# Second mixer of an encoder: queries, keys and values by seven products of half matrices

## The chip, the cores and the metric
One core of a Trainium2 chip runs the whole program. The metric is the device time of one execution in microseconds. Five instruction streams work side by side: PE (TensorE), DVE (VectorE), ACT (ScalarE), POOL (GpSimd) and SP (SyncE, which here only issues DMAs). Each runs its own instructions in order, and semaphores tie them together.

## What is computed
Two token sequences of 512 and 256 tokens (plus 16 meta tokens each, so T = 800 columns) go through two layers: an mLSTM mixer and a SwiGLU network, then a differential attention mixer and a second SwiGLU network. The part that matters here is the attention mixer (8 heads, two components of 64 each):

```python
proj = xn @ w_in                                  # xn = rmsnorm(h), 1024 -> 3 * 1024
q = proj[..., :1024].reshape(B, L, 8, 2, 64); k = proj[..., 1024:2048].reshape(B, L, 8, 2, 64)
v = proj[..., 2048:].reshape(B, L, 8, 128)
q = partial_rope(_rms_f32(q, g_q), cos, sin) * 64 ** -0.5
k = partial_rope(_rms_f32(k, g_k), cos, sin)
p = softmax(q @ k.T);  a = p[:, :, 0] - lam * p[:, :, 1]
o = _rms_f32(a @ v, g_sub) * (1.0 - lambda_init)
h = h + o @ w_out
```

All matrices are float32. The kernel writes each as a rounded high part plus a low part and makes every product three times (high by high, high by low, low by high).

## The kernel before
Activations lie transposed in on-chip memory: `h` holds the residual as 8 tiles of 128 features by 800 tokens. `xh`, `xl` are the high and low parts of the normalised input, `wh`, `wl` those of a block of weights, `sx` the operands of the SwiGLU products. SwiGLU networks (`ffn`) already multiply by a seven-product scheme on half matrices: a product of two halves feeds two outputs, sums of weights are formed in DRAM ahead of time by copies (SP, `copy_for_sum`) and accumulating DMAs (POOL, `add_for_sum`), and sums of activations by DVE. The matmuls of these products are those of L974. `ORDER` is the list of the network's products; the last 28 of the first network belong to four output jobs a, b, c, d of 9 matmuls a product, and DVE adds each to `h` (`add_out`, L1715). When a tile of `h` is complete, ACT writes `xh` and a square (`high_and_square`, L2384, L2387), DVE writes `xl` and adds the square to a running sum (`low_and_squares`, L1624, L1631).

The second mixer is made of 24 blocks, numbered from `MIX1`: for each head a block of keys, one of queries, one of values (`attn_cols`). A block (`run_block`, matmuls on L884, those of the first block on L1408) is 8 feature tiles times 3 part products times 2 column groups, 48 matmuls: 400 + 400 columns for keys and values, 512 + 256 for queries. SP loads 512 KB of weights for a block, POOL rounds them (L774) and subtracts (L778). `sum_squares(3)` (L899) sums the squares of a token over the features, `invert(3)` (L1502) gives `rstd`, and `evacuate` and `evacuate_inner` (L1478, L1493) multiply it in as they take a block out of PSUM.

`head` exists on PE, DVE and ACT. For head hd PE computes the scores of six query tiles (`attn_scores`, L1280, L1285), turns the probabilities (`turn_attention`, L1302) and multiplies them by the values (`attend`, L1312). Scores are always made one tile ahead, and the blocks of head hd + 1 are cut into pieces of whole feature tiles (6 matmuls each) and laid between these steps (`beside`, 13 places). DVE takes the maximum of a score tile (`maxima`, L2077), ACT the exponentials (`exps`, L2659), DVE combines the two components (`combine`, L2091). In the second half of a head DVE also rotates the queries of the next head (`rope_start`, `rope_end`, L2034 to L2046), scales its keys (`normalise_k`, L2072) and scales the outputs (L2105); `turn_key_roots` (L1244) on PE and the scores of the next head's first tile wait for that. In head 7 the places are filled with output blocks (`OUT1`). Heads 1 to 6 run in a hardware loop of two heads a turn.

## Time and profile before

| | |
|---|---|
| median of three executions | 1862.98 us (1862.71 to 1864.3) |
| span of the profiled execution | 1860.4 us |
| PE busy | 1849.7 us, 99% of the span |
| DVE, ACT, POOL busy | 1235.1, 879.7, 1162.6 us |
| granted TensorE clock | 1.000 in the whole span |
| end of the first SwiGLU network on PE | 905.64 us after the span's start |
| first scores of the mixer (head 0) on PE | 938.06 us |
| one head of the loop | 48.35 us |

Busy time of an engine is the time in which it executes something; PE's matmuls overlap in the trace, since the end of one is drawn after the start of the next, so the pace of PE is read from start to start. The time of day inside the program is given as us from the span's start. A wait of an engine is in square brackets behind a row, with what ended it.

### The profile page before, as it was taken

To read this page: it belongs to the slowest core of one execution; us is meant where nothing else is said; L and a number is where in the kernel's file an instruction comes from. 1 tells how busy PE (TensorE), PEld (TensorE's weight loads), DVE (VectorE), ACT (ScalarE), POOL (GpSimd) and SP (SyncE) were. 2 spreads that over 40 slices of the span, in tenths; PEclk is the share of its full clock that TensorE was granted. 3 is DMA by queue.
4 is the path that set the end of the run, shared out by engine and by line. 5 is a ranking of instruction groups with operands and counts; after the bars stand their busy time and mean duration, and the time that the engine had idled before them with its cause. 6 is when DMAs were issued, how large, how long until landed. Compare 5 with 4: busy or idle time off the path is not lost.

```text
span 1860.4 us, 31456 instructions
## 1 busy us (share of the span) xinstructions
PE 1849.7 (99%) x10845; PEld 1742.0 (94%) x10845; DVE 1235.1 (66%) x2072; ACT 879.7 (47%) x1855; POOL 1162.6 (62%) x1533
## 2 busy tenths in 40 slices
PE   9999999999999999999999999999999999999999
PEld 8888889999999999999988888888889999999998
DVE  6756566768576757576876666666587575756663
ACT  6444343455444445454444444444465454444553
POOL 4453644468687878788843333333558788887885
PEclk9999999999999999999999999999999999999999
DMA  8789997549697977774475666664233535353534
GB/s 270 257 240 237 222 259 173 183 108 228 209 237 238 235 227 218 250 232 118 107 145 121 126 124 124 130 118 91 74 90 110 148 99 157 100 153 101 154 112 133
DMA packets 380153, 309.51 MB, mean 166 GB/s; under 512 B 14395, under 2 KB 322398, under 8 KB 379766
## 3 DMA queue, kind: packets, MB, share of 16 engines
q1 hardware_dynamic: 349472, 237.81, 42.1%
q0 software_dynamic: 28416, 69.21, 20.5%
q8 instruction: 73, 1.20, 0.3%
q10 hardware_dynamic: 2134, 0.82, 0.2%
q14 instruction: 58, 0.48, 0.1%
HBM read 302.16 MB, written 144.04 MB: 240 GB/s over the span
## 4 chain that ended last, share of the span: by engine, by line
PE 91%; DVE 5%; ACT 1%; issue 1%; DMA 1%; POOL 0%; SPq 0%; ACTq 0%; DVEq 0%; POOLq 0%
PE ps L974 51%; PE ps L884 26%; PE ps L1155 3%; PE ps L1312 3%; PE ps L1280 2%; PE ps L1302 1%; PE ps L1130 1%; PE ps L1214 1%; DVE rstd L1502 1%; PE ps L1164 1%; DVE sx L1554 0%; PE ps L1244 0%; DVE mx L2077 0%; DVE gt L1661 0%; DMA wk<-in_x_prompt_dram 0%
## 5 line engine op out<-in xcount | busy, mean ns | idle before, releaser
L974 PE MATMUL ps<-sx,wh 128*128 128x400 f32 (+1 forms) x2044 | 530.3, 340 | 0.9 <-POOL wl L808 0.5
L808 POOL TENSOR_TENSOR wl<-raw,wh 128x256 fp32r<-128x256 f32 (+1 forms) x432 | 355.6, 855 | 97.9 <-ACT wh L2243 96.4
L774 POOL CAST wh<-raw 128x256 fp32r<-128x256 f32 x248 | 102.5, 456 | 450.6 <-PE ps L884 424.9
L974 PEld LDWEIGHTS ps<-sx,wh 128*128 128x128 f32 x2044 | 373.4, 188 | 3.0 <-ACT gt_first L2258 0.9
L974 PE MATMUL ps<-sx,wl 128*128 128x400 f32 (+1 forms) x1022 | 347.6, 340 | 0.0
L808 POOL TENSOR_TENSOR wl<-raws,wh 128x256 fp32r<-128x256 f32 x328 | 283.8, 910 | 84.4 <-ACT wh L2243 84.0
L1715 DVE TENSOR_TENSOR h<-h,ps 128x400 f32<-128x400 f32 (+1 forms) x280 | 154.5, 559 | 131.5 <-PE ps L974 131.4
L974 PE MATMUL ps<-fx,wh 128*128 128x400 f32 (+1 forms) x904 | 235.3, 341 | 0.1
L884 PE MATMUL ps<-xh,wh 128*128 128x512 f32 (+1 forms) x752 | 211.2, 357 | 0.0
L884 PE MATMUL ps<-xl,wh 128*128 128x512 f32 (+1 forms) x752 | 207.3, 349 | 0.0
L778 POOL TENSOR_TENSOR wl<-raw,wh 128x256 fp32r<-128x256 f32 x248 | 198.8, 831 | 5.1
L884 PE MATMUL ps<-xh,wl 128*128 128x512 f32 (+1 forms) x752 | 201.3, 345 | 0.0
L2243 ACT ACTIVATE wh<-raw 128x512 fp32r<-128x512 f32 (+2 forms) x268 | 142.7, 535 | 106.5 <-PE ps L974 92.3
L974 PEld LDWEIGHTS ps<-sx,wl 128*128 128x128 f32 x1022 | 191.9, 188 | 0.0
L2243 ACT ACTIVATE wh<-raws 128x512 fp32r<-128x512 f32 (+2 forms) x202 | 108.5, 538 | 159.0 <-PE ps L974 150.5
L974 PEld LDWEIGHTS ps<-fx,wh 128*128 128x128 f32 x904 | 164.6, 188 | 0.5 <-issue 0.5
L974 PE MATMUL ps<-fx,wl 128*128 128x400 f32 (+1 forms) x452 | 153.7, 340 | 0.0
L974 PE MATMUL ps<-sx,w5h 128*128 128x400 f32 (+1 forms) x532 | 138.3, 341 | 0.3 <-ACT gt L2258 0.3
L884 PEld LDWEIGHTS ps<-xl,wh 128*128 128x128 f32 x752 | 126.2, 188 | 10.2
L884 PEld LDWEIGHTS ps<-xh,wl 128*128 128x128 f32 x752 | 124.5, 188 | 10.8
L884 PEld LDWEIGHTS ps<-xh,wh 128*128 128x128 f32 x752 | 120.6, 189 | 14.5 <-issue 3.8
L808 POOL TENSOR_TENSOR w5l<-raw,w5h 128x256 fp32r<-128x256 f32 x112 | 94.8, 868 | 22.5 <-ACT w5h L2243 22.1
(330 smaller groups left out, 3552.0 us busy)
## 6 DMA issues: line engine op xcount, KB each, us to landing
in_sums<-in_ffn_w_in_dram SPq DMA_DIRECT2D x16, 1536.0 KB, 10.7
raw<-in_sums SPq DMA_DIRECT2D x96, 256.0 KB, 3.0
in_sums<-in_ffn_w_in_dram SPq DMA_DIRECT2D x16, 1280.0 KB, 7.2
raw<-in_ffn_w_in_dram SPq DMA_DIRECT2D x80, 256.0 KB, 3.0
raws<-in_sums SPq DMA_DIRECT2D x80, 256.0 KB, 3.1
raw<-out_sums SPq DMA_DIRECT2D x120, 128.0 KB, 2.6
raws<-in_ffn_w_in_dram SPq DMA_DIRECT2D x52, 256.0 KB, 3.1
raw<-in_m_w_in_dram SPq DMA_DIRECT2D x24, 512.0 KB, 4.8
```

The costliest lines, as they stand in the source:

```text
L774: ins = pool.tensor_copy(wh[:, slot, c], raw[:, slot, c])
L778: ins = pool.tensor_tensor(wl[:, slot, c], raw[:, slot, c], wh[:, slot, c].bitcast(F32), ALU.subtract)
L808: ins = pool.tensor_tensor(slot_of(n, 1)[:, c], raw_of(n)[:, c], slot_of(n, 0)[:, c].bitcast(F32), ALU.subtract)
L884: mm = pe.matmul(out, w[:, slot, k * P:(k + 1) * P], x[:, k, a:b], start=(k + q == 0), stop=(k == k_tiles - 1 and q == 2), skip_group_chec ...
L974: mm = pe.matmul(product_bank(layer, s, j), slot_of(n, low_w)[:, k * P:(k + 1) * P], x, start=(j in OPENS and k + q == 0), stop=(k == tile ...
L1130: mm = pe.matmul(flat(2)[0:tz, base + a:base + a + columns], k[:, 1, t0:t0 + tz], q[:, 0, START[s] + a:START[s] + a + columns], start=(t = ...
L1155: mm = pe.matmul(ps[0:tz, state_bank(i) + d, 0:M_DV + 2], w, v, start=(j == js[0] and t == 0), stop=(j == js[-1] and t == len(passes) - 1) ...
L1164: mm = pe.transpose(flat(2)[:, c * 1024 + t0:c * 1024 + t0 + tz], hn(i)[0:tz, c * P:(c + 1) * P], ident[0:tz, 0:tz])
L1280: return pe.matmul(both[:, c, a:b], wk[rows, odd, i * P:(i + 1) * P], wk[rows, 2 + odd, START[s] + a:START[s] + b], start=True, stop=True)
L1312: mm = pe.matmul(acc_o, at[:, i % 2, q, :], va[:, odd, j, :], start=(q == 0), stop=(j == js[-1]), skip_group_check=True)
L1715: ve.tensor_tensor(part, part, product_bank(layer, s, j), ALU.add if result_of(s, j)[0] >= 4 else ALU.subtract).then_inc(out_read, 1)
L2243: sc.activation(slot_of(n, 0)[:, 0:columns], raw_of(n)[:, 0:columns], ACT.Copy).then_inc(prod_hi, 1)
```

## The change
Queries, keys and values of the second mixer are now made by the seven-product scheme too. A **job** is seven products `0, 3, 2, 1, 5, 4, 6` (`KV_ORDER`) of 4 feature-tile pairs times 3 part products, 84 matmuls of 400 columns. A key-value job makes keys and values of one head, a query job the queries of two heads. So there are 8 + 4 jobs, 84 products and 1,008 matmuls for the 24 blocks and 1,152 matmuls.

Around that: `h` tiles are turned into seven high and seven low operands a pair (`mix_part` on ACT and DVE, which takes the place of `high_and_square` and `low_and_squares`; the operands go to `sx`); all eight tiles of `h` are stored to DRAM (`keep_last`) and come back before the output projection, and their room is used for queries, attention tiles and outputs; products leave PSUM by ACT copies (`mix_copy`) and DVE adds (`mix_add`) without `rstd`; the token norm goes into an epsilon term of the key and query norms (`token_scales`, `token_roots`, `eps_sums`) and into the values as ACT copies them (`values`, now eight copies of 128 columns instead of three). The sums of the weights are formed in DRAM by eight copies and eight accumulating DMAs during the first network. POOL makes low parts of 512 columns a product. The outputs of heads 0 to 5 stay in `h` and are split into high and low parts in head 7 (`split_y` on ACT and DVE, six tiles), where DVE's `deliver` of each head was before. The loop over heads is written out. The two jobs of head 0 are made in full ahead of the attention, followed by products 0 and 3 of the next key-value job.

```diff
+KV_ORDER = (0, 3, 2, 1, 5, 4, 6)
...
+def made_in(hd):
+    i, steps = query_pair(hd + 2), [("kv", hd + 1, j) for j in KV_ORDER]
+    if hd % 2 == 0 and hd + 3 < D_HEADS:
+        return [*steps[0:6], ("q", i, 0), steps[6], ("q", i, 3), ("q", i, 2), ("q", i, 1)]
+    if hd % 2:
+        i = query_pair(hd + 1)
+        return [*steps[0:6], ("q", i, 5), steps[6], ("q", i, 4), ("q", i, 6)]
+    return steps
...
+def freed_by(kind, i, j):
+    if split_query(kind, i):
+        return {0: ("kv", 2 * i - 1, 5), 3: ("kv", 2 * i - 1, 6), 2: ("q", i, 0), 1: ("q", i, 2),
+                5: ("kv", 2 * i, 5), 4: ("q", i, 5), 6: ("q", i, 4)}[j]
+    if j in (2, 1, 5, 4, 6):
+        return kind, i, {2: 0, 1: 3, 5: 1, 4: 2, 6: 4}[j]
+    if kind == "q" or i == 0:
+        return None
+    if i == 1:
+        return "kv", 0, {0: 6, 3: 5}[j]
+    if i % 2 == 0:
+        return "q", query_pair(i), {0: 3, 3: 1}[j]
+    return {0: ("kv", i - 1, 6), 3: ("q", query_pair(i - 1), 6)}[j]
...
+HALVES = {"even": (2, 2, 1, 3, 2, 4, 2, 2, 1, 1, 0, 1, 1), "odd": (2, 2, 1, 3, 2, 4, 2, 2, 0, 1, 0, 1, 0),
+          "first": (1, 1, 1, 2, 2, 3, 2, 2, 1, 1, 0, 1, 1), "short": (2, 2, 1, 3, 2, 2, 2, 0, 0, 0, 0, 0, 0)}
...
+            def mix_factor(m):
+                (kind, i, j), which = MIX_ORDER[m], int(MIX_ORDER[m][0] == "q")
+                if m < 4:
+                    sp.wait_ge(prod_split, NF - MIX_RAW_FREE[m])
+                else:
+                    sp.wait_ge(mix_split, m - 3)
...
+                sp.dma_start(mix_raw(m).rearrange("p (k c) -> p k c", k=KP), mix_source(kind, i, j))\
+                  .then_inc(mix_raw_in[m % 4], 16)
...
+            def keep_last(p):
+                sp.wait_ge(sq_ready, KT + 2 * p + 2)
+                for m in (p, p + KP):
+                    sp.dma_start(h_last_kept[:, m, :], h[:, m, :]).then_inc(h_last_stored, 16)
...
-            for n in range(3 * D_HEADS):
-                if n < 2:
-                    sp.wait_ge(prod_split, (NF - 5, NF)[n])
-                weights(MIX1 + n, n % 2, attn_cols(n % 3, (n // 3) * P))
+            for m in range(4):
+                mix_factor(m)
+                if m == 1:
+                    keep_last(0)
+                    keep_last(1)
+            keep_last(2)
+            for m in range(4, N_MIX):
+                mix_factor(m)
+                if m == 5:
+                    keep_last(3)
+                if m in LATER_COPIES:
+                    copy_for_sum(1, LATER_COPIES[m])
+            sp.wait_ge(mix_split, N_MIX)
...
+            def mix_parts(m):
+                if m >= N_FIRST:
+                    pool.wait_ge(mix_raw_in[m % 4], 16 * (m // 4 + 1))
+                    pool.wait_ge(mix_done, m - 3)
+                    for c in pieces(KP * P):
+                        ins = pool.tensor_copy(mix_weight(m, 0)[:, c], mix_raw(m)[:, c])
+                    ins.then_inc(mix_hi, 1)
+                pool.wait_ge(mix_hi, m + 1)
+                for c in pieces(KP * P):
+                    ins = pool.tensor_tensor(mix_weight(m, 1)[:, c], mix_raw(m)[:, c], mix_weight(m, 0)[:, c].bitcast(F32),
+                                             ALU.subtract)
+                ins.then_inc(mix_split, 1)
...
+            def mix_product(x, k0=0, k1=KP, small=()):
+                (kind, i, j), m, small = x, MIX_PLACE[x], list(small)
+                if k0 == 0:
+                    before = freed_by(kind, i, j)
+                    if before is None:
+                        pe.wait_ge(out_read, RANK[41, 3] + 1)
+                    elif before in COPY_RANK:
+                        pe.wait_ge(mix_copied, COPY_RANK[before] + 1)
+                    else:
+                        pe.wait_ge(mix_added, ADD_RANK[before] + 1)
+                    pe.wait_ge(mix_split, m + 1)
+                for p in range(k0, k1):
+                    if m < N_FIRST:
+                        pe.wait_ge(axl_ready, ONCE + NPROD * p + j + 1)
+                    for q, (low_w, low_x) in enumerate(((0, 0), (0, 1), (1, 0))):
+                        mm = pe.matmul(ps[:, mix_bank(kind, i, j), 0:HT], mix_weight(m, low_w)[:, p * P:(p + 1) * P],
+                                       sx[0][:, p * NPROD + j, low_x, :], start=(mix_opens(kind, i, j) and p + q == 0),
+                                       stop=(p == KP - 1 and q == 2), skip_group_check=True)
+                        for f in small[:1]:
+                            f()
+                        del small[:1]
+                if k1 == KP:
+                    mm.then_inc(mix_done, 1)
+                return small
...
+            def token_norms():
+                pe.wait_ge(out_read, N_OUT)
+                pe.wait_ge(sq_summed, 2 * KT)
...
+            for m in range(N_FIRST - 1):
+                small = key_sums(0) if m == 9 else query_sums(0) if m == N_FIRST - 2 else ()
+                for f in mix_product(MIX_ORDER[m], small=small):
+                    f()
+                if m == 5:
+                    token_norms()
...
+            def mix_part(i):
+                p, second = divmod(i, 2)
+                done, sums, c = NPROD * p, 4 * p, KT + i
+                a, b = slice(0, HT), slice(HT, T)
+                def low(j, src):
+                    ve.wait_ge(axh_ready, ONCE + done + j + 1)
+                    ve.tensor_tensor(sx[0][:, p * NPROD + j, 1, :], src, sx[0][:, p * NPROD + j, 0, :].bitcast(F32),
+                                     ALU.subtract).then_inc(axl_ready, 1)
+                ve.wait_ge(axf_ready, ONCE + i + 1)
+                if not second:
+                    ve.tensor_tensor(an1[:, :], axe[:, a], axe[:, b], ALU.subtract).then_inc(atx_ready, 1)
+                    low(B11, axe[:, a])
+                    low(T1, an1[:, :])
+                else:
+                    ve.wait_ge(atx_ready, ONCE + sums + 1)
+                    ve.scalar_tensor_tensor(an2[:, :], an1[:, :], -1.0, axo[:, b], ALU.mult, ALU.subtract).then_inc(atx_ready, 1)
+                    ve.tensor_tensor(axe[:, b], axo[:, b], axe[:, b], ALU.subtract).then_inc(atx_ready, 1)
+                    low(T2, an2[:, :])
+                    low(B21, axo[:, a])
+                    ve.wait_ge(atx_ready, ONCE + sums + 2)
+                    ve.scalar_tensor_tensor(axo[:, a], an2[:, :], -1.0, axo[:, a], ALU.mult, ALU.subtract).then_inc(atx_ready, 1)
+                    ve.wait_ge(atx_ready, ONCE + sums + 3)
+                    low(T3, axe[:, b])
+                    low(B22, axo[:, b])
+                    ve.wait_ge(atx_ready, ONCE + sums + 4)
+                    low(T4, axo[:, a])
                 ve.wait_ge(sq_ready, c + 1)
-                ve.wait_ge(sq_summed, c)
                 if i == 0:
-                    ve.tensor_copy(wk[:, 3, :], wk[:, 4, :]).then_inc(sq_summed, 1)
+                    ve.tensor_copy(rstd[:, :], asq[:, :]).then_inc(sq_summed, 1)
                 else:
-                    ve.tensor_tensor(wk[:, 3, :], wk[:, 3, :], wk[:, 4, :], ALU.add).then_inc(sq_summed, 1)
...
+            def mix_add(x):
+                kind, i, j = x
+                ve.wait_ge(mix_done, MIX_PLACE[x] + 1)
...
+                for dst, a, b in parts:
+                    src = ps[:, mix_bank(kind, i, j), a:b]
+                    if j in (3, 5):
+                        ins = ve.tensor_tensor(dst, src, dst, ALU.add)
+                    else:
+                        ins = ve.scalar_tensor_tensor(dst, src, -1.0, dst, ALU.mult, ALU.subtract)
+                ins.then_inc(mix_added, 1)
...
+            def token_scales():
+                end = 2 * (NQ + NT - 1)
+                for x in (e2, rt):
+                    ve.memset(x[:, :], 1.0).then_inc(small_set, 1)
+                ve.wait_ge(small_set, ONCE + 2)
+                ve.wait_ge(norm_sum, 3)
+                for rows, a, b in ((P, 0, end), (META, end, end + 2)):
+                    ins = ve.tensor_scalar(e2[0:rows, a:b], square_sums[0:rows, a:b], D_HD * EPS / D, D_HD * EPS * EPS,
+                                           ALU.mult, ALU.add)
+                ins.then_inc(e2_ready, 1)
+                ve.wait_ge(norm_root, 3)
+                ve.reciprocal(rt[:, :], rt[:, :]).then_inc(rt_ready, 1)
...
+            kx, qx = keys(0), queries(0)
+            mix_add(("kv", 0, 3))
+            lambda_sums()
+            token_scales()
+            rope_tables()
+            mix_add(("kv", 0, 5))
+            ve.wait_ge(mix_added, ADD_RANK["kv", 0, 5] + 1)
             rope_start(1, kx)
-            evacuate_inner(MIX1 + 1, 1, qx, False)
...
+            def mix_high(m):
+                if m < 4:
+                    sc.wait_ge(prod_done, NF - MIX_FREE[m])
+                else:
+                    sc.wait_ge(mix_done, m - 3)
+                sc.wait_ge(mix_raw_in[m % 4], 16 * (m // 4 + 1))
+                sc.activation(mix_weight(m, 0), mix_raw(m), ACT.Copy).then_inc(mix_hi, 1)
...
+            def split_y(k):
+                sc.wait_ge(yh_ready, YL_OUT[0] + k + 1)
+                sc.wait_ge(mix_done, N_MIX)
+                sc.activation(y_home(k, 0)[:, 0:TQ], h[:, Y_TILE[k], 0:TQ], ACT.Copy).then_inc(split_high, 1)
...
+            sc.wait_ge(h_last_stored, IN_ONCE + 16 * KT)
+            for m in range(N_FIRST - 4):
+                mix_high(m + 4)
+                if not added(*MIX_ORDER[m]):
+                    mix_copy(MIX_ORDER[m])
+                if m == 5:
+                    token_roots()
+                if m == 6:
+                    squares_of(keys
```

Three places show what moved. The first is **DVE at the end of the first network**, before (`xl` and the running sum for a pair of tiles, after the adds of the last two products):

```order
L1715 TENSOR_TENSOR h<-h,ps 128x400 [waits out_read,prod_done] x2
L1624 SCALAR_TENSOR_TENSOR xl<-h,par,xh 128x800 [waits xh_ready]
L1631 TENSOR_TENSOR wk<-wk 128x800 [waits sq_summed,sq_ready]
L1715 TENSOR_TENSOR h<-h,ps 128x400 [waits out_read,prod_done] x2
L1624 SCALAR_TENSOR_TENSOR xl<-h,par,xh 128x800 [waits xh_ready]
L1631 TENSOR_TENSOR wk<-wk 128x800 [waits sq_summed,sq_ready]
L1624 SCALAR_TENSOR_TENSOR xl<-h,par,xh 128x800 [waits xh_ready]
L1631 TENSOR_TENSOR wk<-wk 128x800 [waits sq_summed,sq_ready]
```

and now (`an`, `axe`, `axo` are the sums of the halves, `mrow_masked` is the semaphore that counts ACT's high parts, `gate_soft` and `gate_m` that of its scaled tiles and of the sums):

```order
L2043 TENSOR_TENSOR h<-h,ps 128x400 [waits out_read,prod_done] x2
L1922 TENSOR_TENSOR an<-axe 128x400 [waits gate_soft]
L1917 TENSOR_TENSOR sx<-axe,sx 128x400 [waits mrow_masked]
L1917 TENSOR_TENSOR sx<-an,sx 128x400 [waits mrow_masked]
L1943 TENSOR_TENSOR rstd<-rstd,asq 128x800 [waits sq_summed,sq_ready]
L1927 SCALAR_TENSOR_TENSOR an<-an,axo 128x400 [waits gate_m,gate_soft]
L1928 TENSOR_TENSOR axe<-axo,axe 128x400
L1917 TENSOR_TENSOR sx<-an,sx 128x400 [waits mrow_masked]
L1917 TENSOR_TENSOR sx<-axo,sx 128x400 [waits mrow_masked]
L1932 SCALAR_TENSOR_TENSOR axo<-an,axo 128x400 [waits gate_m]
L1917 TENSOR_TENSOR sx<-axe,sx 128x400 [waits mrow_masked,gate_m]
L1917 TENSOR_TENSOR sx<-axo,sx 128x400 [waits mrow_masked]
```

The last two adds stand behind the second part of the pair before, and a pair has 13 instructions of its own on DVE instead of 4 (the last two of it stand below these rows).

The second is **ACT between the last tile of the network and the first copy out of PSUM**, before:

```order
L2384 ACTIVATE xh<-h,par 128x800 [waits out_read]
L2387 ACTIVATE wk<-h 128x800 [waits sq_summed]
L2448 ACT_TABLE_LOAD
L2448 ACTIVATE lam<-lam 128x2 [waits lam_sums]
L2228 ACT_TABLE_LOAD
L2228 ACTIVATE rstd<-ps,small 128x800 [waits norm_sum]
L2632 ACTIVATE spare<-wk 128x800 [waits acc_free]
L2632 ACTIVATE spare<-wk 128x768 [waits acc_free]
L2638 ACTIVATE qk<-ps,small 128x26 [waits qks_done]
```

and now (`h_first_stored` counts the stores of `h`):

```order
L2805 ACTIVATE asq<-h 128x800 [waits sq_summed]
L2737 DMA ck<-in_rope_dram 128x528
L2738 DMA sk<-in_rope_dram 128x528
L2743 DMA lv<-in_d_lam_q_dram 128x64 [waits prod_split]
L2743 DMA lv<-in_d_lam_k_dram 128x64
L2743 DMA lv<-in_d_lam_q_dram 128x64
L2743 DMA lv<-in_d_lam_k_dram 128x64
L2752 ACTIVATE wh<-raw 128x512 [waits mix_raw_in0,mix_done,h_first_stored]
L2763 ACTIVATE wk<-ps 128x400 [waits mix_done]
```

The first copy of a product, L2763, stands behind all parts of all tiles and behind a wait for the last store of `h`.

The third is **DVE behind the first key-value job**, before:

```order
L1615 TENSOR_TENSOR lam<-lam 128x1 [waits lam_exp]
L1618 TENSOR_SCALAR lam<-lam 128x1 [waits vstep]
L1502 RECIPROCAL rstd<-rstd 128x800 [waits norm_root]
L2024 MEMSET qk 128x28 [waits rstd_ready]
L1478 TENSOR_TENSOR wk<-ps,rstd 128x800 [waits block_done,attn_set]
L2034 STREAM_SHUFFLE spare<-wk 128x800 [waits acc_free,vstep]
L2037 TENSOR_TENSOR spare<-spare,sk 128x528 [waits vstep]
L2037 TENSOR_TENSOR spare<-spare,sk 128x272
```

and now (`norm_sum` is given by PE behind the job's sixth product, `norm_root` by ACT):

```order
L1882 MEMSET kd 128x64
L1885 STREAM_SHUFFLE gswap<-par 128x2 [waits h_back]
L1886 TENSOR_SCALAR cq<-ck,par 128x528
L1887 TENSOR_SCALAR gsub<-par 128x1
L1889 TENSOR_SCALAR ck<-ck,par 128x528 [waits attn_set]
L1890 TENSOR_SCALAR sq<-sk,gswap 128x528
L1892 TENSOR_SCALAR sk<-sk,gswap 128x528 [waits attn_set]
L1956 TENSOR_TENSOR wk<-ps,wk 128x400 [waits mix_copied,mix_done]
L2369 STREAM_SHUFFLE swapped<-wk 128x800 [waits mix_added,vstep]
L2372 TENSOR_TENSOR swapped<-swapped,sk 128x528 [waits vstep]
L2372 TENSOR_TENSOR swapped<-swapped,sk 128x272
L1958 SCALAR_TENSOR_TENSOR v_raw<-ps,v_raw 128x400 [waits mix_copied,mix_done]
```

The add of product 4 into `v_raw` (L1958) stands behind the tables and the first half of the key rotation. PE's row for product 6, which goes to the same PSUM bank, stands behind the token norms and waits for that add:

```order
L1482 MATMUL ps<-sx,wl 128x400
L1504 MATMUL ps<-ones,rstd 128x2 [waits sq_summed,out_read]
L1504 MATMUL ps<-ones,rstd 128x2 x12
L1504 MATMUL ps<-ones,rstd 16x2
L1482 MATMUL ps<-sx,wh 128x400 [waits gates_done,mix_split,mix_added]
L1482 MATMUL ps<-sx,wh 128x400
```


## Rows read from the trace of the kernel before

**Rows 1.** The page's head, and the clock, PE's longest wait (waited for: us, times, longest).
```profile
span 1860.4 us, 31456 instructions
PE 1849.7 (99%) x10845; PEld 1742.0 (94%) x10845; DVE 1235.1 (66%) x2072; ACT 879.7 (47%) x1855; POOL 1162.6 (62%) x1533
...
core 0: 1860.4 us, clock 1.000
...
PE ps L1034 <- DVE ones L1772: 1.1, 1, 1.1
```

**Rows 2.** Stretches: length, PE, PEld, DVE, ACT, POOL busy, clock, DMA share, GB/s.
```profile
1029.50:1077.90 48.40, 48.28 (x305) 41.52 (x306) 32.36 (x72) 22.12 (x60) 17.39 (x27) 1.00 0.68 132
```

**Rows 3.** Timeline of PE: start us, us, line and operation, count.
```profile
905.64 0.53 PE L1408 MATMUL ps<-xh,wh 128*128 128x400 f32 x2
...
938.06 1.13 PE L1280 MATMUL ps<-wk 64*128 64x512 f32 x4
...
1045.51 0.53 PE L884 MATMUL ps<-xh,wl 128*128 128x400 f32 x2
1045.87 0.53 PE L884 MATMUL ps<-xh,wh 128*128 128x400 f32 x2
...
1055.34 0.51 PE L884 MATMUL ps<-xh,wl 128*128 128x512 f32 x2
1055.69 0.51 PE L884 MATMUL ps<-xh,wh 128*128 128x512 f32 x2
...
1060.53 0.28 PE L1214 MATMUL ps<-cst,spare 128*128 128x2 f32 x2
1060.67 0.47 PE L884 MATMUL ps<-xh,wl 128*128 128x512 f32 x1
```

**Rows 4.** Timeline of DVE, end of the first network and its start.
```profile
399.64 0.57 DVE L1577 SCALAR_TENSOR_TENSOR tx<-tx,xo 128x400 f32<-128x400 f32 x1 [1.04 <-ACT xo L2308]
...
401.65 1.11 DVE L1554 TENSOR_TENSOR sx<-xo,sx 128x400 fp32r<-128x400 f32 x1
...
877.92 0.57 DVE L1715 TENSOR_TENSOR h<-h,ps 128x400 f32<-128x400 f32 x1 [1.06 <-PE ps L974]
```

**Rows 5.** Groups of instructions: count, busy us, mean ns, idle before.
```profile
L778 POOL TENSOR_TENSOR wl<-raw,wh 128x256 fp32r<-128x256 f32 x248 | 198.8, 831 | 5.1
...
L1554 DVE TENSOR_TENSOR sx<-xo,sx 128x400 fp32r<-128x400 f32 (+1 forms) x24 | 18.3, 790 | 0.0
...
L1631 DVE TENSOR_TENSOR wk<-wk 128x800 f32<-128x800 f32 x7 | 9.2, 1310 | 0.0
```

**Rows 6.** Timeline of ACT: scaled tile, table load.
```profile
398.64 0.97 ACT L2308 ACTIVATE xo<-h,par 128x800 f32<-128x800 f32 x1 [0.39 <-DVE h L1508]
...
914.12 1.28 ACT L2228 ACT_TABLE_LOAD   x1
```

**Rows 7.** DMA issues: queue, count, KB each, us to landing.
```profile
h_first_kept<-h SPq DMA_DIRECT2D x1, 800.0 KB, 5.8
```

**Rows 8.** Timeline of DVE ahead of head 0: tables, reciprocal, first rotation.
```profile
913.94 0.82 DVE L1599 TENSOR_SCALAR cq<-ck,par 128x528 f32<-128x528 f32 x1
...
916.22 0.52 DVE L1605 TENSOR_SCALAR sk<-sk,gswap 128x528 f32<-128x528 f32 x1
...
923.63 1.11 DVE L2034 STREAM_SHUFFLE spare<-wk 128x800 f32<-128x800 f32 x1
924.77 1.30 DVE L2037 TENSOR_TENSOR spare<-spare,sk 128x528 f32<-128x528 f32 x2
```

**Rows 9.** Timeline of one head's second half, PE's rows and DVE's.
```profile
1063.48 0.73 PE L1280 MATMUL ps<-wk 64*128 64x272 f32 x4
...
1076.45 0.31 PE L1285 MATMUL ps<-kd,wk 128*128 128x32 f32 x2
...
1064.52 0.71 DVE L2077 TENSOR_REDUCE mx<-ps 128x2 f32<-128x544 f32 x1
...
1075.28 0.46 DVE L2072 TENSOR_TENSOR wk<-ps,wk 128x288 f32<-128x288 f32 x1
```

661 lines of the change are left out of this document (431 added, 230 removed).

## The prediction
> **What bounds the kernel now.** First the page's head: PE is busy for 99% of the span and its longest wait is 1.1 us, so PE's own work is the bound, at a granted clock of 1.000 throughout [rows 1]. Then the stretches: one head takes 48.4 us, PE is busy in all of it and DVE for 32.4 us [rows 2]. Then PE's timeline, read from start to start: two matmuls of 400 columns take 0.366 us, so one takes 0.183; a pair of 512 + 256 takes 0.35, so one takes 0.175; a sum into 2 columns, two rows of the trace, takes 0.14 [rows 3]. The first network ends at 905.64 and the first scores start at 938.06, with PE full between [rows 3]. Less work on PE is therefore worth its full time only where the others keep up. The last view is the second half of a head: from the end of the scores of tile 4 (1064.2) DVE works without a break from 1064.52 to 1075.74, and PE starts the next head's scores at 1076.45, 0.7 us later [rows 9]. There DVE is as long as PE is.
>
> **What the products save.** Before, 768 matmuls of 400 columns and 384 of 384 on average: 768 x 0.183 + 384 x 0.175 = 207.7 us. After, 1,008 x 0.183 = 184.5. The saving is 23.2 us. New small matmuls: 14 token sums for the four matmuls of `sum_squares` (about 2.0 for 1.0 us) and 8 `eps_sums`, 1.1 us: 2.1 us back.
>
> **The end of the first network.** The last products of the network come every 1.64 us, and DVE's add takes 0.57 with 1.07 idle [rows 4]. From start to start I take 0.49 for an add or a difference on 400 columns, and for the subtraction that makes a low part 0.72, since its mean is 790 ns [rows 5], between 0.57 for a difference and 1.11 beside POOL [rows 4]. The running sum takes 1.2 [rows 5]. First tile of a pair: 0.49 + 2 x 0.72 + 1.2 = 3.15 us; second: 3 x 0.49 + 5 x 0.72 + 1.2 = 6.3. Four pairs are 38 us on DVE, where the time from the add at 877.92 to the network's end is 27.7 us, which also holds 17 adds, 8.3 us. DVE falls behind. I walked it: pair 0 ends 888.9, pair 1 901.3, pair 2 914.5, the last two adds 915.5, then ACT scales tile 7 (0.87), and pair 3 gives its first low part at 917.2, the low parts of its second tile between 921.0 and 924.4. ACT's last square ends at 923.6 (ACT's scaling of a tile shows 0.97 us [rows 6]; start to start I take 0.87, and 0.45 for half a tile). PE is slowed at once, since product c6 needs the bank that the add of c4 frees (901.8 instead of 893): the network ends at 910.1, 4.5 us late.
>
> **The first key-value job.** Product 0 runs three of its four pairs and waits for 917.2: 5.4 us. Product 3 waits for its low part until 921.7: 2.3 us, and ends at 922.3. Product 2 needs product 0's copy, which ACT makes only when all of `h` is stored. SP sees the last square at 923.6; a store of 800 KB took 5.8 us to land [rows 7], and I take 5.2 for two tiles, so 928.8; one weight part and the copy, 929.8. PE waits 7.6 us. Product 5 follows product 1 in the same bank and waits for its copy, 1.1 us. Product 4 ends at 939.8, the token norms at 941.8. Then PE needs the add of product 4, and before that add stand, one behind the other: the epsilon terms 0.5, ACT's table load 1.28 [rows 6] and roots 0.3, the tables 2.8 (913.94 to 916.7), the add of product 5 0.5, shuffle and sine product 2.3 [rows 8], the add 0.5, and some 0.4 for handing over: 8.6 us, to 950.4. What is queued behind product 6 on PE is all of the query job. That job costs its products, 1.5 us of sums, and two waits more, for the copy of product 1 (1.0) and for the key roots (1.3): turns done at 973.7, products 0 and 3 of the next job end at 978.1. DVE has the rotated queries at 974.2, the keys at 975.8. The first scores start at 978.2 instead of 938.06: **40.1 us later**. Ahead of them lie 192 matmuls where 138 were, 9.9 us; so some 30 of these 40 us are waits and late work.
>
> **The heads.** Behind the first scores lay 678 matmuls of 400 columns and 336 of 384 before, 182.9 us; now 68 products, 816 matmuls, 149.3 us: 33.6 us less, and 1.0 more for `eps_sums`. The cover gets thinner just where DVE is full. From scores 4 to the next head's scores DVE needs, as before, 11.2 us, starts 0.3 earlier since no query block is evacuated, and has one add more, 0.5: keys ready 11.7 us after 1064.2, at 1075.9 on the old clock. PE had 30 block matmuls there. Heads 2 and 4 have 24 (arrival 1.1 us earlier, 1075.3), heads 1, 3, 5 have 18 (2.2 earlier, 1074.2), head 6 none (5.5 earlier, 1070.9). The waits are 0.7, 1.8 and 5.1 us. In head 6 PE then also waits 1.1 for the last combination, having nothing between. In head 0 product 5 comes straight behind product 1, and its copy stands behind two sets of exponentials: about 2.3 us, and 1.2 in its second half. In head 7 output block 0 needs `split_y`: PE arrives 0.9 us after scores 1, but maximum, exponentials, ACT's copy and DVE's subtraction take 5.0, and the fourth tile waits once more behind `values`: 6 us. Sum: 2 x 0.7 + 3 x 1.8 + 6.2 + 3.5 + 6 = 22.5 us. Nothing in the trace shows the loop's cost apart, so I take writing it out at 0; POOL's subtractions, 84 x 2 x 0.831 = 140 us [rows 5], and the shorter roundings fit beside some 400 us.
>
> **The sum**, against the span of 1860.4: 40.1 - 33.6 + 1.0 + 22.5 = **+30.0 us**, 1890.4. The median lies 2.6 us above the span, so 1893.
>
> Of the low parts, the row beside POOL is twice as long as that of a difference [rows 4]. The Trainium skill (GPSIMD Engine Reference, 1. Specifications) says that GpSimd shares its access with VectorE where a VectorE instruction has two inputs there; by this rule the low parts, made while POOL splits weights, would all go at the slow rate, 28 times 0.3 us more, and the first scores would come 8 us later. The trace's mean says that they take turns.
>
> **The rivals.** (a) **PE stays fed**, the result is faster: DVE keeps up at 0.57 a low part and the store and table steps run under other work. Nothing moves but PE's work: -23.2 + 2.1 = -21, 1842. It decides from the point where all waits together are under 21 us; my walk has 30 + 22. Against it is the order, in which each step named stands behind the other on one engine. (b) **Only the front costs**: DVE in the heads takes less than the rows of the old head show, and only head 7's 6 us stay: 40.1 - 33.6 + 1 + 6 = +13.5, 1876. (c) **The clock falls.** The clock is 1.000 throughout, and PE never waited over 1.1 us [rows 1], so the trace can't price it; now waits of 5.4, 7.6 and 8.6 us come. If after each one product ran at 1.2 GHz instead of 2.4, 2.2 us more each: +6.6, 1900. The Trainium skill (TensorE: Matmul & The Clock Gate, Part 1) says that an idle array falls back to half its clock and needs activity to regain it, which speaks for (c). (d) **POOL and DVE disturb each other** in the heads, where POOL's 17 us a head [rows 2] grow with the columns that it splits, 84 x 512 for 24 x 1,024, 1.75 times: 10% on 31 us of DVE, a third of it on the path, in eight heads +8, 1901.
>
> **How the numbers follow.** Forecast as summed 45%, (b) 20%, (c) 15%, (d) 10%, (a) 7%, no change 3%. The forecast's own bounds: low parts at 0.55 or 1.0 us move the front by -5 to +8, the store by -1.5 to +1, the heads' 22.5 may be 12 to 30: 1874 to 1910. That range takes in (b), (c) and (d). A measurement of this kernel tells 0.2%, 4 us, from no change. Faster 0.08, same 0.03, slower 0.89.
>
> **What would show it.** Right: PE idle for over 20 us between 907 and 980, with waits on DVE's low parts, on ACT's first copy and, longest, on the add of product 4; first scores near 978; idle of 1 to 2 us at each odd head's end, about 6 us at the end of head 6 and again early in head 7. Granted clock under 1.00 in the front would show (c). Wrong: first scores ahead of 960, or heads of 44.5 and 46.7 us without waits, which is what their products alone give.

## The result, and the profile after

| | kernel before | kernel changed |
|---|---|---|
| median | 1862.85 us (1862.45 to 1864.3, 4 runs) | 2007.22 us (2003.3 to 2009.58, 4 runs) |
| ratio | | 1.0772, 95% interval 1.0756 to 1.0787 |
| span of the profiled execution | 1860.4 us | 2001.2 us |

The forecast was 1893 us, with a range of 1874 to 1910. The sign was right and the size was not: +144 us instead of +30. The page of the changed kernel answers to [rows 1]:

```profile
span 2001.2 us, 31398 instructions
...
PE 1884.7 (94%) x10741; PEld 1766.9 (88%) x10741; DVE 1254.4 (63%) x2120; ACT 926.1 (46%) x1989; POOL 1252.9 (63%) x1661
...
PE   9999999989968899999679899999899999999999
...
PEclk9999999999988989999778999997999999999999
DMA  7899996398899998743478978662333354443534
```

PE worked 99% of the span before and works 94% now, though its products are fewer. In the 40 slices of 50 us PE and its clock have holes together in the twelfth and thirteenth and at the twentieth and twenty-first, and the DMA row stands at 8 and 9 from the ninth to the sixteenth, most of the first network. The next rows are stretches of the changed kernel (columns as in [rows 2]: length, busy time of PE, PEld, DVE, ACT, POOL, granted clock, DMA share, GB/s): the first network, the front up to the first scores, head 3 and head 6.

```profile
core 0: us, PE busy (x) PEld busy (x) DVE busy (x) ACT busy (x) POOL busy (x), PEclk, DMA share, GB/s
397.00:966.30 569.30, 522.91 (x2782) 516.66 (x2782) 352.20 (x459) 255.10 (x499) 411.58 (x490) 0.96 0.81 213
966.30:1044.00 77.70, 54.58 (x260) 51.14 (x259) 30.95 (x68) 25.08 (x47) 36.52 (x50) 0.76 0.61 165
...
1199.90:1249.70 49.80, 45.98 (x289) 39.53 (x289) 33.30 (x73) 25.24 (x74) 30.50 (x46) 1.00 0.87 173
...
1348.10:1400.00 51.90, 47.51 (x250) 39.32 (x251) 31.11 (x67) 24.20 (x68) 19.42 (x30) 0.81 0.25 51
```

I divide the span at three rows of PE: the start of the first network's last matmul, the first scores, and the first product of the second network. What lies behind the third mark takes 496.6 us in both kernels. All times below come from these marks.

| stage | before | forecast | changed | of it PE's waits | lost by the clock |
|---|---|---|---|---|---|
| first network ends at | 905.5 | 910.1 | 966.1 | 46 | 15 |
| front, to the first scores | 32.6 | 68.1 | 78.2 | 23.1 | see below |
| heads, to the second network | 425.7 | 415.6 | 460.3 | 37.9 | 29 |

In the network the row 397:966 has 46.4 us in which PE isn't busy; its busy time is 14.8 us above that of the same products before (508.1), at a clock of 0.96. The 29 us are the sum of (1 - clock) times length over the ten stretches of the heads. 60.6 + 45.6 + 34.6 = 140.8 us, the whole difference of the spans. So there are three differences to explain: 56 us in the first network that the forecast did not have at all, 10 us in the front, and 45 us in the heads.

**The network's waits.** Groups of PE rows, with the idle time before them and what ended it:

```profile
L1234 PE MATMUL ps<-sx,wh 128*128 128x400 f32 (+1 forms) x2044 | 535.4, 343 | 30.3 <-ACT gt L2623 28.3 <-POOL wl L1074 1.6 <-DVE ut L1976 0.2
...
L1234 PE MATMUL ps<-fx,wh 128*128 128x400 f32 (+1 forms) x904 | 238.7, 345 | 12.1 <-POOL wl L1074 11.8 <-issue 0.2
L1482 PE MATMUL ps<-sx,wh 128*128 128x400 f32 x672 | 209.3, 385 | 32.7 <-DVE v_raw L1958 17.0 <-ACT wk L2763 7.1 <-DVE sx L1917 4.7
```

Before, the first of these groups had 0.9 us of idle time:

```profile
L974 PE MATMUL ps<-sx,wh 128*128 128x400 f32 (+1 forms) x2044 | 530.3, 340 | 0.9 <-POOL wl L808 0.5
```

The longest single wait is one of 17.77 us at 586.93, and behind it stands a DMA. The rows are, in turn: SP's issues (start, length of the issue), ACT's rounding of the weights, PE, and for the stretch 553 to 578 us the DMA queues (packets, MB, share of 16 engines) and the landing times (count, KB each, median us).

```profile
556.55 0.57 SPq L883 DMA_DIRECT2D raw<-in_sums  x1
...
565.37 11.68 SPq L883 DMA_DIRECT2D raws<-out_sums  x1
...
585.01 0.63 ACT L2608 ACTIVATE wh<-raw 128x512 fp32r<-128x512 f32 x1 [19.30 <-DMA raw<-in_sums]
...
586.93 1.03 PE L1234 MATMUL ps<-sx,wh 128*128 128x400 f32 x2 [17.77 <-ACT gt L2623]
...
q0 software_dynamic: 935, 3.59, 72.1%
q1 hardware_dynamic: 3150, 2.65, 35.6%
...
kv_sums<-in_d_w_in_dram POOLq DMA_DIRECT2D x2, 2048.0 KB, 18.0
...
raw<-in_sums SPq DMA_DIRECT2D x1, 256.0 KB, 28.4
```

SP asks for 256 KB of weights at 556.55 and they land 28.4 us later; such a load takes 3.1 us in the median of the whole program, and 4.5 us in the first network of the kernel before. Meanwhile POOL's queue q0 runs two accumulations of 2 MB, forming the sums for keys and values, and takes 72.1% of the DMA time for 3.59 MB, while SP's queue q1 gets 35.6% for 2.65 MB. A later issue on SP, which takes 0.4 us in the median, holds SP for 11.68 us. By these rows an accumulated MB costs 1.5 times a copied one (3.59 / 0.721 against 2.65 / 0.356). The Trainium skill (DMA: Bandwidth & Descriptors, Queues, rings and completion order) says that each DMA engine goes round between the queues that have work for it, a packet at a time. The rows agree in that q1 is not shut out: it gets a share, and all that stands in it, copies and loads, shares that. That the turns are even they do not show, with 935 packets of q0 to 3,150 of q1.

### The profile page after: what moved, and what is told of

Its sections match the earlier page's. It is cut to its first block and busy times, and to the rows that moved or that the text cites. A ratio compares the mean times of both kernels' runs of the same rounds, so it can differ in the third digit from the quotient of the medians.

```text
span 2001.2 us, 31398 instructions
## 1 busy us (share of the span) xinstructions
PE 1884.7 (94%) x10741; PEld 1766.9 (88%) x10741; DVE 1254.4 (63%) x2120; ACT 926.1 (46%) x1989; POOL 1252.9 (63%) x1661
## 5 line engine op out<-in xcount | busy, mean ns | idle before, releaser
L1234 PE MATMUL ps<-sx,wh 128*128 128x400 f32 (+1 forms) x2044 | 535.4, 343 | 30.3 <-ACT gt L2623 28.3
L1234 PEld LDWEIGHTS ps<-sx,wh 128*128 128x128 f32 x2044 | 376.3, 190 | 34.4 <-ACT gt L2623 30.2
L1482 PE MATMUL ps<-sx,wh 128*128 128x400 f32 x672 | 209.3, 385 | 32.7 <-DVE v_raw L1958 17.0
L1012 POOL CAST wh<-raw 128x256 fp32r<-128x256 f32 x156 | 66.5, 473 | 269.5 <-PE ps L1149 187.4
L1482 PEld LDWEIGHTS ps<-sx,wh 128*128 128x128 f32 x672 | 128.1, 202 | 41.2 <-DVE v_raw L1958 19.1
L1065 POOL TENSOR_TENSOR wl<-raw,wh 128x256 fp32r<-128x256 f32 x168 | 131.1, 801 | 40.8 <-ACT wh L2752 35.1
L1061 POOL CAST wh<-raw 128x256 fp32r<-128x256 f32 x140 | 63.8, 510 | 142.7 <-PE ps L1482 121.3
L1016 POOL TENSOR_TENSOR wl<-raw,wh 128x256 fp32r<-128x256 f32 x156 | 129.1, 856 | 3.2
L1482 PE MATMUL ps<-sx,wl 128*128 128x400 f32 x336 | 125.3, 373 | 0.0
L3081 ACT ACTIVATE wk<-ps,nb,qkr 128x528 f32<-128x528 f32 (+1 forms) x96 | 68.3, 717 | 91.7 <-DVE nb L2414 91.6
```

Of the source, the lines that this page charges most:

```text
L1012: ins = pool.tensor_copy(wh[:, slot, c], raw[:, slot, c])
L1016: ins = pool.tensor_tensor(wl[:, slot, c], raw[:, slot, c], wh[:, slot, c].bitcast(F32), ALU.subtract)
L1061: ins = pool.tensor_copy(mix_weight(m, 0)[:, c], mix_raw(m)[:, c])
L1065: ins = pool.tensor_tensor(mix_weight(m, 1)[:, c], mix_raw(m)[:, c], mix_weight(m, 0)[:, c].bitcast(F32), ALU.subtract)
L1234: mm = pe.matmul(product_bank(layer, s, j), slot_of(n, low_w)[:, k * P:(k + 1) * P], x, start=(j in OPENS and k + q == 0), stop=(k == tile ...
L1482: mm = pe.matmul(ps[:, mix_bank(kind, i, j), 0:HT], mix_weight(m, low_w)[:, p * P:(p + 1) * P], sx[0][:, p * NPROD + j, low_x, :], start=( ...
```

## The experiments

e1 and e2 leave sums out, and e10 spoils one running sum (last section); all other kernels compute what the reference does. The times are medians; the table gives PE's marks of the profiled execution (network's end, length of the front, length of the heads), in us.

| kernel | time | network's end | front | heads |
|---|---|---|---|---|
| changed | 2007.2 | 966.1 | 78.2 | 460.3 |
| e1 no sums formed | 1956.2 | 911.4 | 81.1 | 470.6 |
| e2 copies, no accumulations | 1964.1 | 917.7 | 78.0 | 470.4 |
| e3 sums spread | 1976.7 | 936.7 | 78.5 | 460.4 |
| e4 before, with the sums | 1925.9 | 963.5 | 32.2 | 425.5 |
| e5 order of the front | 1995.7 | 968.9 | 62.0 | 460.1 |
| e6 front filled | 2005.5 | 965.4 | 76.6 | 463.5 |
| e7 product 4 added first | 1979.3 | 967.6 | 79.3 | 438.1 |
| e8 sums and copies spread | 1984.9 | 947.8 | 78.2 | 458.1 |
| e9 = e5 + e7 + third spreading | 1937.2 | 934.9 | 65.9 | 436.7 |
| e10 = e9 filled | 1928.2 | 933.9 | 67.0 | 429.5 |
| e11 = e9, small accumulations | 1935.3 | 927.6 | 70.4 | 437.8 |
| e12 = e11 filled | 1929.4 | 935.6 | 69.4 | 431.9 |
| e16 = e12, front wholly filled | 1925.6 | 926.9 | 66.4 | 435.1 |

### The first network: e1 to e4

e1 leaves the sixteen DMAs out, e2 the eight accumulations, e3 moves them, e4 adds them to the kernel before:

```diff
-MIX_COPIES = {1: 0, 2: 1, 3: 2, 4: 3, 6: 4, 7: 5, 8: 6, 9: 7}
-MIX_ADDS = {(12, 0): 0, (13, 0): 1, (15, 0): 2, (17, 0): 3, (20, 0): 4, (21, 0): 5, (23, 0): 6, (25, 0): 7}
+MIX_COPIES = {}                                                # e1
+MIX_ADDS = {}                                                  # e1, e2
+MIX_COPIES = {1: 0, 4: 1, 7: 2, 17: 3, 26: 4, 27: 5, 34: 6, 35: 7}    # e3
+MIX_ADDS = {(23, 0): 0, (25, 0): 1, (29, 0): 2, (33, 0): 3, (36, 0): 4, (37, 0): 5, (39, 0): 6, (41, 0): 7}    # e3
```

> The changed kernel without the eight copies and eight accumulating DMAs that form the weight sums of the second mixer; the products that want a sum read plain weights instead, so queries, keys and values are other numbers; all else stays. Theory A (the 57 us that the first network lost beyond the forecast are weight loads that stand behind these 24 MB): the network ends near 909 us instead of 966.3, PE's waits before 900 us are gone, and the time is 2007 - 57 = 1950 us. Theory B (the loss has another cause, for instance the copies for the second network that now start later, or POOL's work): the network still ends beyond 950 and the time stays above 1990.

> The changed kernel with the eight copies but without the eight accumulating DMAs: the sums hold one addend only, so queries, keys and values are other numbers. The profile shows three of the five longest waits of the network (17.8, 8.0 and 4.5 us at 587, 625 and 734 us) while accumulations run and one (5.4 us at 445) while copies run. If the accumulations are the main part, some 45 of the 57 us go: network end near 921, time near 1962. If copies and accumulations weigh alike by bytes (12 MB each), about half goes: network end near 938, time near 1979. If neither is the cause, 2007.

> The changed kernel with the same sixteen DMAs, computing the same, but spread over the network: copies behind the loads of hidden tiles and output jobs 1, 4, 7, 17, 26, 27, 34, 35 instead of 1 to 9, accumulations at 23, 25, 29, 33, 36, 37, 39, 41 instead of 12 to 25. Theory A1 (the place decides: too much is queued at once between 410 and 750 us, while the DMA share is under 0.5 from 850 on): most of the 57 us come back, network end 915 to 930, time 1956 to 1975. Theory A2 (the volume decides, wherever it lies): network end above 950 and time above 1990.

> The kernel before, computing what it did, with the sixteen DMAs of the changed kernel added at the same places of the first network; nothing uses what they form, and its own 24 copies for the second network all stay in the first (the changed kernel has 16 of them there). Theory A (the DMAs alone cost it): the network ends 57 us later or more, near 965 instead of 905.6, time 1920 to 1935 with the rest unchanged. Theory B (they don't): 1863 to 1870.

Without the DMAs the network ends at 911.4, 5.9 us behind the kernel before and 1.3 behind the forecast. The group of PE that had 30.3 us of idle time has 0.9 again:

```profile
L1228 PE MATMUL ps<-sx,wh 128*128 128x400 f32 (+1 forms) x2044 | 530.5, 341 | 0.9 <-POOL wl L1068 0.5 <-DVE ut L1970 0.2
```

The time is 1956.2 instead of the expected 1950, because the heads of its profiled execution were 10 us longer than the changed kernel's; nothing in them differs from the changed kernel, and the section on the clock returns to this. With the copies alone the network ends at 917.7: copies cost 6 us, accumulations on top of them 48 of the 55. How much of the 48 comes from their kind and how much from where they lie, no run separates. And in the kernel before, where nothing uses the sums, the same DMAs move the network's end from 905.5 to 963.5 and the time by 3.4% (1.0341, interval 1.0324 to 1.0358), with the front and heads unchanged to 0.4 us. Its rows:

```profile
L1017 PE MATMUL ps<-sx,wh 128*128 128x400 f32 (+1 forms) x2044 | 535.9, 343 | 16.7 <-ACT gt L2301 14.4 <-POOL wl L849 2.0 <-DVE ut L1691 0.2
...
L1017 PE MATMUL ps<-fx,wh 128*128 128x400 f32 (+1 forms) x904 | 240.0, 347 | 15.4 <-POOL wl L849 15.1 <-issue 0.2
```

Theory A is shown from both sides. Spreading (e3) brings back 29 of the 55 us, less than theory A1 expected and more than A2.

### The front: e5 and e6

```diff
+            rope_tables()
+            mix_add(("kv", 0, 5))
+            mix_add(("kv", 0, 4))
             token_scales()
-            rope_tables()
-            mix_add(("kv", 0, 5))
...
-            mix_add(("kv", 0, 4))
...
-            sc.wait_ge(h_last_stored, IN_ONCE + 16 * KT)
             for m in range(N_FIRST - 4):
+                if m == 7:
+                    sc.wait_ge(h_last_stored, IN_ONCE + 16 * KT)
```

> The changed kernel, computing the same, with two steps of the front in another order: ACT waits for the stores of the residual only ahead of the first copy that writes into its room (the first query product) and not ahead of the first copy of the key-value job; DVE makes the tables and the adds of products 5 and 4 before the token scales. Theory A (both waits stand where the forecast put them, and the low clock follows them): the waits of 7.1 us at product 2 and 6.5 us at product 6 fall below 2 us each, the stretches at 1.2 GHz behind them go too, the front (last matmul of the first network to first scores, 78.2 us) takes 50 to 58 us, the time is 2007 - 24 = 1983 us. Theory B (the work of DVE and ACT as a whole bounds the front, the waits only change place): the front stays above 70 us and the time above 1998.

> The changed kernel, computing the same, with matmuls whose result nobody reads laid where PE waits in the front: 26 of 400 columns (4.8 us) ahead of the last feature pair of product 0, 38 (7.0 us) ahead of product 2, 35 (6.4 us) ahead of product 6. Nothing that PE waited for comes earlier. Theory C (the clock fell because PE stood still, and the fall costs by itself): the granted clock of the front, 0.76, rises above 0.95; the front is 35.1 us of products, about 4 of small matmuls and 23 of waits, 62 to 65 us instead of 78.2; the time is 2007 - 15 = 1992 us. Theory D (the clock falls for another reason, or the slow matmuls lie in time that would be waited anyway): the front stays at 75 to 78 us.

In e5 the wait at product 2 fell from 7.1 to 3.3 us, that at product 6 is gone, and the front takes 62.0 us, the upper end of theory A's range plus 4. The heads and the network are as before, and the single times scatter from 1989 to 2011, so the median (1995.7) shows only 11.5 of the 16. In e6 the clock was 1.00 from the network's end to 1000 us (0.50 to 0.78 in the four stretches of 5 us from 970 to 990 of the changed kernel), but product 2 began 20.4 us behind the network's end, where it had been 19.1, and the front took 76.6. That spoke for theory D, or for a front bounded by DVE and ACT; e13 to e16 take it up. The clock fell later in this front, to 0.67 from 1000 to 1005 us, though PE was busy all of that time.

### The heads: e7

```diff
+                    add("kv", 4)
                     rope_end(1, kx, hd + 1)
-                    add("kv", 4)
```

> The changed kernel, computing the same; in the heads DVE adds product 4 before it ends the rotation of the keys and not behind it. In the profile product 6 waits for this add in seven heads, 10.6 us in all, which the forecast had left out. Theory A (the order on DVE makes this wait): the waits for v_raw in the heads fall from 10.6 to under 2 us, those for the key roots grow by 0.4 us a head at most, and heads that had no other wait become 1.2 to 1.5 us shorter; time 2007 - 7 = 2000 us, less still if the low clock behind these waits goes. Theory B (DVE is full there, so that the wait comes back at the key roots): the heads stay at 460 us, time 2003 to 2010.

The heads became 22.2 us shorter, against 9.5 us less waiting (37.9 to 28.4). The time fell by 28 us, where theory A said 7. The waits on `v_raw` are gone and those for the key roots hardly grew. Totals of PE's waits in the heads (engine, line, what it waited for: us, times, longest), first of the changed kernel, then of e7:

```profile
PE ps L1482 <- DVE v_raw L1958: 10.6, 7, 2.0
PE ps L1552 <- DVE key_roots L2387: 7.5, 5, 3.4
PE ps L1149 <- DVE ya L2455: 6.2, 2, 4.3
```

```profile
PE ps L1552 <- DVE key_roots L2387: 8.6, 7, 2.1
PE ps L1149 <- DVE ya L2455: 5.7, 2, 4.3
```

The other 12.7 us are the clock: the sum of (1 - clock) times length over e7's heads is 15, against 29.

### More spreading, the repairs together, small accumulations: e8, e9, e11

> The changed kernel, computing the same, with the sixteen DMAs for the sums of the second mixer spread as in the run before and the sixteen copies for the second network spread too, one or two for each ten microseconds up to the end of the network, so that accumulations of 2 MB and copies meet less. If only the crowd in time matters, the network ends at 912 to 925 us (e1: 911.4 with none of the sixteen DMAs, the first spreading: 936.7) and the time is 1952 to 1966. If the sum of bytes bounds, it ends near 937 again.

> The changed kernel, computing the same, with the three repairs together: the front's order (first run of it: front 62.0 us for 78.2), product 4 added before the rotation ends (heads 438.1 us for 460.3), and a third spreading of the sixteen DMAs, by the DMA share in ten microsecond steps of the kernel without them: copies of 2 MB where it is 0.27 to 0.6 (460 to 520 us), the rest and six accumulations from 695 us on, the last one behind the third product of the mixer. Theory A (the three causes are separate and add up): network end 920 to 930, front 62, heads 438, time 1995 - 40 to 50 - 22 or from the other side 1976.7 - 16 - 22 = 1939, 1930 to 1945. Theory B (they share one resource, the slack of the DVE or the clock): the gains of front and heads shrink by half, 1955 to 1965. Neither reaches the kernel before.

> The kernel of e9 (front order, product 4 first), computing the same, with each of the four accumulations of 2 MB cut into four of 512 KB, one behind the first low part of sixteen different tiles or output jobs from 13 to 33, and the accumulations for the queries issued at 34, 35 and 37, so that POOL's issues of 2.8 us leave the network's end. In the changed kernel a weight load of 256 KB took 28.4 us to land while two accumulations of 2 MB ran (their queue held 72% of the DMA time of that stretch, 553 to 578 us). Theory A1 (a burst of 2 MB keeps the loads out; small ones let them through): the network, which ended at 934.9 us in e9, ends at 914 to 922 and the time is 1937 - 15 to 20 = 1917 to 1922. Theory A2 (the sum of bytes decides): it ends at 930 to 940, the time is 1932 to 1942; POOL's sixteen more issues of 1 us could even add to it.

e8 was a miss: the network ended at 947.8, later than in e3, with waits of 7.0 and 7.8 us at 598 and 715 us; accumulations had moved there. e9 puts the repairs together and gave 1937.2, inside theory A's 1930 to 1945: the causes add up, though the network's end (934.9, expected 920 to 930) and the front (65.9, expected 62) came out later. e11 cuts each accumulation of 2 MB in four:

```diff
+KV_PIECES = (13, 14, 15, 16, 17, 20, 21, 22, 24, 25, 27, 28, 30, 31, 32, 33)
+MIX_ADDS = {**{(s, 0): i for i, s in enumerate(KV_PIECES)}, (34, 0): 16, (35, 0): 17, (37, 0): 18}
```

The network ends at 927.6, between the two theories, with no wait over 2.4 us in it, but the front was 4.5 us longer than in e9 (waits of 16.0 us for 13.1, a clock of 0.81 for 0.84; why, no run tells) and the time about the same, 1935.3. The queues of e11 in 397 to 930 us:

```profile
q1 hardware_dynamic: 141234, 96.79, 60.2%
q0 software_dynamic: 17840, 23.07, 27.1%
```

Together 87% of 16 engines over 533 us. What is left, 927.6 against 911.4, fits the volume; that is argued and not shown.

### The clock: e10, e12, e13 to e16

In e10, e12 and e16 PE makes small matmuls that nobody reads where it would wait (`filler`, 0.23 us each):

```diff
+            def filler(n, bank=7):
+                for _ in range(n):
+                    pe.matmul(ps[:, bank, HT:512], ones[:, :], ones[:, 0:512 - HT], start=True, stop=True,
+                              skip_group_check=True)
```

> The kernel of the run before it with matmuls of 112 columns that nobody reads laid into seven waits of PE: 20 ahead of the last pair of product 0, 14 ahead of product 2, 7 ahead of product 1, 7 ahead of the first turn of the key roots, 14 ahead of the second scores of head 0, 18 and 6 in the first output block of head 7. The first filling left the front at 76.6 us, since the clock, kept at 1.00 through the filled waits, fell later, behind unfilled waits of 1.4 and 1.6 us. Theory C (it is standing still that brings the clock down, wherever): with these filled too the mean clock of the front and of heads 0 and 7 is over 0.95, and the time is 10 to 20 us under the run before. Theory D (the fall comes by another rule, and filling only moves it): the time is within 5 us of the run before.

> The kernel of the run before it, computing the same, with filling matmuls as in e10, but without the 6 in the middle of the output block: those started a new sum in other columns of the PSUM bank in which PE was still adding up the second sequence's half of the block, and e10's second output was not that of the reference. Theory C (filling keeps the clock): 7 to 10 us under the run before, as e10 was 9.0 under e9. Theory D: no difference over 3 us.

e10 is 9.0 us under e9 and e12 5.9 under e11, where a wait that is filled is not shortened. Both lie between their theories. The gain is in the heads (7.2 and 5.9 us); the front is 1.1 us longer and 1.0 shorter. For a clean price, e13 to e15 make one wait ahead of the first scores of the kernel before, where PE waits nowhere else (25 copies of ACT; e14 puts 20 `filler` matmuls in front of it; e15 has 16 copies):

```diff
             key_query_roots(0)
+            for k in range(25):
+                sc.activation(junk, ones[:, :], ACT.Copy).then_inc(stall, 1)
+                sc.wait_ge(stall, k + 1)
             exps(0, 0, 0)
```

> The kernel before, computing the same, in which ACT makes 25 small copies one after the other ahead of the first exponentials and PE waits for the last of them ahead of the first scores of the mixer: one idle wait of PE of about 5 us (3 to 7), where the kernel has none. Theory C (a wait brings the clock down and so costs more than its length): the granted clock falls to 0.5 for some 10 us behind the wait, and the time grows by the wait and 3 to 7 us more: 1863 + 5 + 5 = 1873. Theory D (one wait costs its length): the clock stays at 1.00, or falls only while PE stands still, and the time grows by the length of the wait, 1868.

> The same wait with 20 matmuls of 112 columns in front of it whose result nobody reads, 0.23 us each as in the filled runs, 4.6 us in all; what PE waits for comes at the same moment. Theory C: the clock stays at 1.00, and the time is that of the kernel before and the wait alone, 1868, 3 to 7 us under the run before it. Theory D: the same time as the run before it.

> The same with 16 copies instead of 25: an idle wait of 1.5 to 2 us, like those of the heads. In the profile of the changed kernel such waits were followed by half the clock in some places (1.6 us at 1180, 2.0 us at 1378) and in others not (2.0 us at 1128, 1.6 us at 1233). Theory C says that a single short one costs its length only or up to 7 us more, by chance from execution to execution: 1865 with single times up to 1872. Theory D: 1865 in all.

> The kernel of e12, computing the same, with the filling of the front completed: 23 ahead of the last pair of product 0, 7 ahead of that of product 3, 17 ahead of product 2, 16 ahead of product 1, 3 ahead of the query job's third product, 5 ahead of its token sums. In e12 a wait of 2.35 us stayed at product 1, the clock fell behind it, and the front took 69.4 us against 70.4 without filling. Theory C: with no idle wait over 1 us in the front its mean clock is over 0.97 and it takes 35 us of products, 4 of small matmuls and 16 to 20 of waits, 56 to 60 us, so the time is about 10 us under e12's. Theory B (DVE and ACT bound the front, and PE at half clock merely fills time that would be waited): the front stays at 66 to 70 us though the clock is up.

The idle wait was 4.49 us long, and PE ran at the level of 1.2 GHz in part of the 10 us from its end on. Rows of e13, PE's and stretches, then of e14:

```profile
943.08 0.64 PE L1286 MATMUL ps<-kd,wk 128*128 128x32 f32 x2 [4.49 <-ACT wk L2735]
...
940.00:945.00 5.00, 1.92 (x6) 1.01 (x6) 0.00 (x0) 2.77 (x9) 4.14 (x6) 0.66 0.45 93
945.00:950.00 5.00, 5.00 (x19) 4.32 (x18) 1.42 (x2) 2.69 (x4) 0.00 (x0) 0.65 1.08 233
950.00:955.00 5.00, 5.00 (x31) 3.92 (x30) 2.58 (x6) 2.54 (x8) 0.00 (x0) 1.00 0.83 159
```

```profile
948.37 0.41 PE L1286 MATMUL ps<-kd,wk 128*128 128x32 f32 x2 [1.10 <-ACT wk L2663]
...
940.00:945.00 5.00, 4.95 (x34) 3.97 (x33) 1.17 (x1) 2.08 (x7) 3.46 (x5) 1.00 0.62 138
945.00:950.00 5.00, 3.90 (x21) 2.77 (x20) 1.52 (x6) 2.94 (x5) 0.00 (x0) 1.00 1.07 201
```

The times are 1869.67 us (1869.16 to 1870.41) idle and 1868.20 (1867.66 to 1868.71) filled: no single time of the one reaches the other. So the fall costs 1.5 us on top of this wait, where theory C said 3 to 7. One reason stands in the rows: e14 arrives earlier at the next scores and waits 1.10 us there, which e13 doesn't. The short waits of e15 (1.42 and 1.23 us) left the clock at 1.00 and cost about their length: 1865.8, 3.0 us above the 1862.8 of the kernel before.

e16 fills the front until only 2.5 us of idle waits are left. Stretches of the front of e11, then of e16:

```profile
930.00:997.00 67.00, 51.41 (x245) 48.56 (x246) 30.01 (x64) 22.84 (x43) 37.16 (x50) 0.80 0.78 204
```

```profile
930.00:997.00 67.00, 64.40 (x425) 61.52 (x423) 31.40 (x68) 23.99 (x46) 40.27 (x54) 0.97 0.81 213
```

The clock went from 0.80 to 0.97 and the front from 70.4 to 66.4 us, where theory C expected 56 to 60 and theory B 66 to 70. The length is theory B's, but that DVE and ACT are the bound at this length is not shown. e5, in the same order and without any filling, has a front of 62.0 us at a clock of 0.92. In e16 sixteen fillers (3.7 us) stand ahead of product 1, where PE had no wait in e11, and product 5 begins 25.5 us behind the network's end, 23.3 in e5. So the filling itself may hold PE up, and what a full clock alone would give stays open.

The clock also fell once where PE did not wait. The last wait ahead of it (1.11 us) ended at 952.38; then came products and 3.1 us of sums into 2 columns. Row of PE, and stretches:

```profile
956.88 3.09 PE L1527 MATMUL ps<-ones,rstd 128*128 128x2 f32 x28
...
960.00:962.00 2.00, 2.00 (x10) 2.00 (x11) 1.45 (x5) 0.40 (x2) 0.00 (x0) 0.83 0.48 134
962.00:964.00 2.00, 2.00 (x8) 1.98 (x7) 1.08 (x3) 0.86 (x2) 0.15 (x1) 0.50 0.03 8
```

So idle time is not all that the clock follows; no run here takes these small sums apart from it. e16 is the fastest kernel with the change, 1925.6 us (1.0333 of the kernel before, interval 1.0317 to 1.0348), 3.8 us under e12, where theory C said about 10. No version reached the kernel before.

## Why the prediction was wrong

**The step that failed is one that it doesn't have: the sums of the weights.** The prediction prices products, small matmuls, DVE, ACT, waits, POOL's subtractions and the store of `h`; the eight copies and eight accumulations that the section on the change names got no term. They cost 55 us (966.1 against 911.4), half of the miss of 114. They could have been priced from the trace of before. These are the queues of the first network there (packets, MB, share of 16 engines):

```profile
q1 hardware_dynamic: 134999, 94.11, 61.1%
q0 software_dynamic: 4736, 11.53, 13.0%
```

POOL's accumulations take 1.13% of the DMA time a MB, SP's copies and loads 0.65%. The change adds 12.6 MB of each kind and takes eight copies out of the network (11.5 MB): 14.2 + 8.2 - 7.5, 15 points more on a share of 0.75. A mean of 0.90 looks as if it fits. But the copies are issued at 394 to 501 us and the accumulations at 555 to 738, and in e1, without them, the share of most stretches of 10 us from 410 to 460 and from 520 to 680 is 0.8 to 1.1 already, while 460 to 520 and 790 to 905 stand at 0.17 to 0.62.

**The end of the first network: the number was right by luck.** +4.5 us were forecast and +5.9 measured in e1, but the way was another one. The prediction lets product c6 wait for an add; in e1 the wait is for weights. DVE is late with a difference, ACT stands behind it with the rounding of weights queued, POOL behind ACT, and PE behind POOL (rows of ACT, POOL and PE):

```profile
898.25 0.54 ACT L2770 ACTIVATE sx<-axo 128x400 fp32r<-128x400 f32 x1 [1.21 <-DVE axo L1926]
...
900.04 2.65 POOL L1068 TENSOR_TENSOR wl<-raws,wh 128x256 fp32r<-128x256 f32 x4 [2.74 <-ACT wh L2602]
...
901.73 1.00 PE L1228 MATMUL ps<-fx,wh 128*128 128x400 f32 x2 [2.37 <-POOL wl L1068]
```

**The front: the waits were right one by one, their consequence wasn't.** Rows of PE in the changed kernel, with the waits:

```profile
972.87 1.03 PE L1482 MATMUL ps<-sx,wh 128*128 128x400 f32 x2 [4.74 <-DVE sx L1917]
...
985.22 1.04 PE L1482 MATMUL ps<-sx,wh 128*128 128x400 f32 x2 [7.12 <-ACT wk L2763]
...
1007.54 1.04 PE L1482 MATMUL ps<-sx,wh 128*128 128x400 f32 x2 [6.46 <-DVE v_raw L1958]
...
1034.49 1.12 PE L1552 MATMUL ps<-cst,key_roots 128*128 128x128 f32 x4 [1.60 <-DVE key_roots L2387]
```

| wait | forecast | measured |
|---|---|---|
| last pair, product 0 | 5.4 | 4.7 |
| low part, product 3 | 2.3 | under 0.5 (0.6 in e2, e11) |
| store and copy, product 2 | 7.6 | 7.1 |
| copy, product 1's bank | 1.1 | 1.1 |
| add of product 4, product 6 | 8.6 | 6.5 |
| query job, copy | 1.0 | 0.6 |
| query sums | none | 1.4 |
| key roots | 1.3 | 1.6 |

That is 27.3 forecast and 23.0 measured. Yet the front took 78.2 us instead of 68.1, since the clock fell to a mean of 0.76. This is rival (c), to which the prediction gave 15% and 6.6 us. In the front it is worth the 10 us by which the stage missed and the 4 by which the waits were shorter than forecast: 14 us. In e16, which fills the waits, 4 us of them came back. With the order of e5 the front takes 62.0 us in e5, 65.9 in e9 and 70.4 in e11, so the order of two steps is worth 8 to 16.

**The heads: one wait missing, and the clock.** The saving of 33.6 us is there: in e7 the heads take 438.1, of which 28.4 are waits and 15 the clock, which leaves 394.7 for work, where 425.7 - 33.6 + 1.0 = 393.1 was forecast. Of waits 22.5 us were forecast and 37.9 came. 10.6 of the 15.4 between are one step: product 6 waits for the add of product 4, which DVE makes behind the end of the rotation. The prediction counted this add as 0.5 us of DVE's work in the second half of a head, and never asked who waits for it. The rest fits in sum: key roots, keys and turns 13.1 us (13.0 forecast for heads 1 to 6), head 0 4.2 (3.5), head 7 7.8 (6). In the first of these luck has a part. Only 8.5 of the 13.1 are the waits for key roots and keys that the forecast names: 3.4 in head 1 (1.8 forecast) and 1.9 in head 6 (6.2 forecast; 3.1 in e7). The other 4.6 are short waits ahead of scores and turns that it doesn't have. The other term is the clock, 29 us, forecast at nought. It is down behind some of the waits of 0.6 to 3.6 us in the heads and not behind others. That the waits have a part in it e7 and e10 show: with fewer or filled waits the term is 15 and 7 us. Head 6 is the worst; PE's row, and stretches:

```profile
1378.32 0.64 PE L1482 MATMUL ps<-sx,wh 128*128 128x400 f32 x2 [1.71 <-DVE v_raw L1958]
...
1375.00:1380.00 5.00, 2.75 (x18) 2.15 (x17) 4.26 (x10) 2.57 (x8) 0.00 (x0) 1.00 0.02 3
1380.00:1385.00 5.00, 5.00 (x20) 4.25 (x19) 0.00 (x0) 0.00 (x0) 0.00 (x0) 0.50 0.00 0
...
1400.00:1405.00 5.00, 5.00 (x17) 2.96 (x18) 3.48 (x12) 1.05 (x3) 0.00 (x0) 0.50 1.13 208
...
1410.00:1415.00 5.00, 1.38 (x5) 1.25 (x6) 2.81 (x4) 4.13 (x9) 0.00 (x0) 0.91 0.10 13
```

A wait of 1.71 us (with one of 0.54 ahead of it) is followed by 27 us at half the clock, from 1380 to about 1407. PE is busy in the first 16 of them, then waits 0.86 and 1.00 us, and its work is in good part small sums and turns. The Trainium skill (TensorE: Matmul & The Clock Gate, Part 1) says that the array gets its full clock back after it has been busy again for a while. In the front and in e13 the rows agree, the clock is back within the next 10 us; why it took 27 us in head 6, no run here tells, and that stays open.

How much this part takes varies from run to run: in e1, e2, e3, e6 and e8 the same instructions in the heads took 470.6, 470.4, 460.4, 463.5 and 458.1 us.

**The other rivals.** (a), PE stays fed, and (b), only the front costs, fell with the waits. (d), POOL and DVE disturbing each other, is not seen: in head 3 DVE is busy for 33.3 us where it was 32.4 [rows 2], while POOL went from 17.4 to 30.5. That writing out the loop costs nothing was not tested apart; PE's work of 394.7 us for 393.1 leaves little room for it.

In short: of the 114 us between forecast and result, 55 are the sums, 29 the clock in the heads, 15 more waits there, 10 the front, 1 the network's end, and 3 the scatter between span and median. The forecast's own bounds could not hold that: its low end, by the bounds that it lists, is 1876 rather than 1874, and none of them is for a DMA or, beyond rival (c), for the clock.

## What to carry to other kernels

Give each DMA that a change adds a term of its own, in share of the DMA engines a MB, by queue, from the trace of before, and lay it over the share of the very stretch in which it will run: here the share stood at 0.8 to 1.1 in most of the stretch already, and weight loads came late behind the accumulations, whatever the mean said. Where an engine will wait for another's step, ask what stands ahead of that step in the other's queue and can go behind it; in this kernel such changes of order gave back 8 to 16 us in the front and 22 in the heads, 13 of these by the clock. Where PE is the bound, an idle wait can cost more than its length. Where PE waits for others, fill its waits only after asking what work the filling itself puts off: here it brought 4 us of a front of 70.

## What the runs showed of the hardware

- Accumulating DMAs from DRAM to DRAM took 1.5 to 1.9 times the DMA time of copies and loads for the same bytes (1.5 in 553 to 578 us of the changed kernel, 1.7 in the first network before, 1.9 in that of e11), and with two of them and a copy under way a load of 256 KB landed after 28.4 us; its median is 3.1.
- SP's issue of a DMA takes 0.4 us in the median, and 6.8 at most in the kernel before; while two accumulations ran in the changed kernel one took 11.7 us, and all that stood behind it on SP was late too.
- One idle wait of 4.5 us cost 1.5 us on top of its length (e13, e14), waits of 1.4 and 1.2 us nothing that the times show (e15). In head 6 of the changed kernel PE ran at 1.2 GHz for 27 us in which it waited only 0.86 and 1.00 us, and in e16 the clock fell to 1.2 GHz without a wait, within 2 us of the end of 3.1 us of sums into 2 columns.
- In e10 a `filler` that starts a new sum in columns 400 to 512 of a PSUM bank stood in the middle of a sum in columns 0 to 256 of the same bank, and the output of the second sequence, which this sum feeds, changed by a tenth; that of the first did not, nor did either in e12, which lacks this filler. The Trainium skill (Advanced Engine Details and Errata, PSUM Accumulation) says that a starting matmul clears the marks of what was written in the whole bank, so that the running sum begins anew; the two runs agree with it.
